# Adding the last layer's output into HBM by accumulating transfers instead of on VectorE

## What is computed

```python
h    = rmsnorm(x, g_ple_pre)
gate = sigmoid(h @ w_ple_gate)            # 2048 x 2048
proj = p @ w_ple_proj                     #  256 x 2048
y    = rmsnorm(gate * proj, g_ple_post)
out  = x + y                              # 256 x 2048, fp32, 2 MB
```

## Time and profile before

| what | value |
|---|---|
| median of the runs | 3245.95 us |
| the profiled execution's own time | 3246.77 us |
| its span, first to last instruction | 3244.8 us |
| TensorE busy | 3213.2 us, 99% |
| VectorE busy | 2093.9 us, 65% |
| ScalarE busy | 1584.2 us, 49% |
| GpSimd busy | 88.6 us, 3% |
| moved by DMA | 596.27 MB, mean 184 GB/s |
| mean granted TensorE clock | 0.998 of full speed |

### The profile page before, as it was taken

One profiled execution on the slowest core, in us unless ns is written; L12 is line 12 of the kernel. 1 busy time (PEld: TensorE's weight loads), 2 busy tenths in 40 slices (PEclk: granted clock), 3 DMA queues, 4 the chain that ended last, 5 costly groups with the idle time before them and its releaser, 6 DMA issues.

```text
span 3244.8 us, 50378 instructions
## 1 busy us (share of the span) xinstructions
PE 3213.2 (99%) x19512; PEld 2846.4 (88%) x19512; DVE 2093.9 (65%) x2258; ACT 1584.2 (49%) x1895; POOL 88.6 (3%) x36
## 2 busy tenths in 40 slices
PE   8999999999999999999999999999999999999997
PEld 7899988888888888888888888999988888888886
DVE  6566677766665557665555456867986655554568
ACT  5445556555454445444444435555644444444354
POOL 0000200000000100000000010000010000000101
PEclk9999999999999999999999999999999999999999
DMA  8545555666666556666656555654556666566654
GB/s 265 177 156 171 190 172 173 194 187 185 193 185 192 188 189 187 190 183 192 187 181 197 190 189 164 220 165 128 178 164 188 186 190 187 179 198 193 189 175 134
DMA packets 324345, 596.27 MB, mean 184 GB/s; under 512 B 18436, under 2 KB 46500, under 8 KB 324196
## 3 DMA queue, kind: packets, MB, share of 16 engines
q1 hardware_dynamic: 316048, 587.27, 58.4%
q10 hardware_dynamic: 8148, 6.90, 0.7%
HBM read 591.97 MB, written 2.13 MB: 183 GB/s over the span
## 4 chain that ended last, share of the span: by engine, by line
PE 95%; DVE 3%; ACT 1%; DMA 1%; issue 0%; POOL 0%; ACTq 0%; DVEq 0%; POOLq 0%
PE acc L715 26%; PE acc L717 25%; PE acc L720 24%; PE acc L775 5%; PE acc L778 4%; PE acc L777 4%; DVE WHL L1830 1%; PE acc L660 1%; PE acc L658 1%; PE acc L659 1%; DMA raw<-in_cmp_k_w 0%; PE acc L596 0%; ACT WHL L1219 0%; PE acc L804 0%; PE acc L963 0%
## 5 line engine op out<-in xcount | busy, mean ns | idle before, releaser
L1830 DVE TENSOR_TENSOR WHL<-raw,WHL 128x1024 fp32r<-128x1024 f32 x1112 | 1384.0, 1255 | 971.6 <-ACT WHL L1219 970.5
L1219 ACT ACTIVATE WHL<-raw 128x1024 fp32r<-128x1024 f32 x1112 | 1164.4, 1057 | 1249.8 <-PE acc L720 992.5
L717 PEld LDWEIGHTS acc<-OPR,WHL 128*128 128x128 f32 x4800 | 903.1, 188 | 199.0
L715 PE MATMUL acc<-OPR,WHL 128*128 128x512 f32 x2556 | 999.9, 397 | 10.8 <-DVE WHL L1830 10.1
L717 PE MATMUL acc<-OPR,WHL 128*128 128x256 f32 x4800 | 971.2, 278 | 0.0
L720 PE MATMUL acc<-OPR,WHL 128*128 128x512 f32 x2244 | 888.3, 396 | 0.0
L715 PEld LDWEIGHTS acc<-OPR,WHL 128*128 128x128 f32 x2556 | 485.5, 190 | 27.9 <-issue 11.3
L717 PEld LDWEIGHTS acc<-HR,WHL 128*128 128x128 f32 x2184 | 410.3, 188 | 94.5
L715 PE MATMUL acc<-HR,WHL 128*128 128x512 f32 x1120 | 440.3, 395 | 0.0
L717 PE MATMUL acc<-HR,WHL 128*128 128x256 f32 x2184 | 433.9, 278 | 0.0
L720 PE MATMUL acc<-HR,WHL 128*128 128x512 f32 x1064 | 420.9, 396 | 0.0
(11 more groups left out here) (390 smaller groups left out, 2288.1 us busy)
## 6 DMA issues: line engine op xcount, KB each, us to landing
raw<-in_w_up SPq DMA_DIRECT2D x176, 512.0 KB, 4.4
raw<-in_ff_w_gate SPq DMA_DIRECT2D x176, 512.0 KB, 3.8
raw<-in_ff_w_up SPq DMA_DIRECT2D x176, 512.0 KB, 4.5
raw<-in_ff_w_down SPq DMA_DIRECT2D x176, 512.0 KB, 4.3
raw<-in_w_in SPq DMA_DIRECT2D x162, 512.0 KB, 4.1
raw<-in_w_down SPq DMA_DIRECT2D x88, 512.0 KB, 3.8
raw<-in_w_out SPq DMA_DIRECT2D x64, 512.0 KB, 4.1
raw<-in_w_ple_gate SPq DMA_DIRECT2D x32, 512.0 KB, 4.8
```

The lines of the kernel that those rows point to most:

```text
L715: pe.matmul(acc[:, b + t, :], wh[:, s, col:col + P], x, start=first, stop=False)
L717: mm = pe.matmul(acc[:, b + t, 0:T], wl[:, s, col:col + P], x[:, 0, :], start=False, stop=last and t % 2 == 0)
L1219: act.activation(wh[:, s, :], raw[:, s, :], ACT.Copy).then_inc(hi_done, 1)
L1830: dve.tensor_tensor(wl[:, s, :], raw[:, s, :], wh[:, s, :].bitcast(F32), ALU.subtract)\
```

## The change

The output gets `X` by one 2 MB transfer, which SP issues between the loads of `ple_gate` and those of `ple_gb` once `X` is final. At the end VectorE only multiplies, in place in `YG`, without the waits on its own results. GpSimd waits for that one store and then, for each group, issues a transfer from `YG` that adds to what the output holds. SP ends the program when the five adding transfers have landed.

```diff
             stream("ple_gate", *plain(a["w_ple_gate_2"]))
+            sp.wait_ge(first_x, 3 * FIRST_X["ple_pre"] + 3)
+            sp.wait_ge(ssq_src, SRC["ple_pre"] + 4)
+            sp.dma_start(out.rearrange("(c p) t -> p c t", p=P), X[:, :, :]).then_inc(out_stored, 16)
             stream("ple_gb", *plain(a["w_ple_gate_2"], 2 * NB))
             stream("ple_pl", *plain(a["w_ple_proj_2"], 3 * NB))
 
-            for n, (first, last) in enumerate(OUT_GROUPS):
-                sp.wait_ge(out_done, n + 1)
-                sp.dma_start(out.rearrange("(c p) t -> p c t", p=P)[:, first:last, :], X[:, first:last, :])\
-                  .then_inc(out_stored, 16)
-            sp.wait_ge(out_stored, 16 * len(OUT_GROUPS))
+            sp.wait_ge(out_added, 16 * len(OUT_GROUPS))
...
             for n, (first, last) in enumerate(OUT_GROUPS):
                 k = last - first
                 dve.wait_ge(y_scaled, first // 4 + 1)
-                if n >= 1:
-                    dve.wait_ge(out_done, n)
-                chain(dve.tensor_tensor(T2[:, 0:k, :], YG[:, first:last, :], bc(RSTD[:, :], k), ALU.mult))
-                dve.tensor_tensor(X[:, first:last, :], X[:, first:last, :], T2[:, 0:k, :], ALU.add).then_inc(out_done, 1)
+                dve.tensor_tensor(YG[:, first:last, :], YG[:, first:last, :], bc(RSTD[:, :], k), ALU.mult)\
+                   .then_inc(out_done, 1)
...
             squares("ple_post", four(HFc, 20, 3), y_done, 1)
+            gp.wait_ge(out_stored, 16)
+            for n, (first, last) in enumerate(OUT_GROUPS):
+                gp.wait_ge(out_done, n + 1)
+                gp.dma_start(out.rearrange("(c p) t -> p c t", p=P)[:, first:last, :], YG[:, first:last, :], accum_op=ALU.add)\
+                  .then_inc(out_added, 16)
```

More of the change, by code:

```diff
@@ L311, in program @@
         pg_pre, pg_sig = sem("pg_pre"), sem("pg_sig")
+        out_added = sem("out_added")
         out_done, y_scaled = sem("out_done"), sem("y_scaled")
```

## The result

The changed kernel takes 3250.53 us, the median of 20 runs between 3249.47 and 3252.28; the kernel before takes 3246.43 us in 20 runs beside them (3245.76 to 3247.36). That is 4.1 us more, a ratio of 1.0013 with a 95% interval of 1.0007 to 1.0018. It is slower, by more than the noise of the comparison but by less than the 6.5 us that the text above counts as a change. The forecast was +3.8 us and 3249.8. The profiled execution took 3249.47 us with a span of 3247.6.

A forecast was written before the change was run, and what follows sets the result against it. VectorE paces the end, the transfers follow. First multiply 3232.75 plus 0.1, 1.8, 0.7, 12.3 and 0.6 gives 3248.2 against 3244.4, or +3.8; early store 0; 3246.0 + 3.8 = 3249.8 us, range 3242 to 3266.

The forecast's parts named there:

- The floor: Kernel's end: last multiply 3236.2 plus 0.1 plus 2.1 us of a small store, -6.0 us at best.
- VectorE's part: Kernel's end: five adds and their waits go; multiplies end 3232.75 to 3236.2, last group ready 6.0 us earlier.
- The start of the block: Adding transfers at the end: after the first multiply, wake-up 0.1, GpSimd's issue 1.8, first packet 0.7, reaching 3235.35.
- The size of the block: Adding transfers at the end: moving the bytes takes 12.3 us, bounded between 6.2 and 36.4 us.
- Two passes: Adding transfers at the end: fetch and write one after the other on each transfer engine, 12.3 us.
- The cover for the issues: GpSimd's later issues hide beside the bytes of earlier ones, up to 3.1 us an issue.
- Rival B: Transfers at the end: adding is as cheap as storing, 6.2 us of bytes; -3.7 us, 3242.3; chance 0.13.
- Rival C: Transfer engines after 3232.85: read-add-write of small rows bound by its own delay; +12.5 to +24.9 us; chance 0.31.
- the likeliest case: Kernel's end: added read halves the rate, adding transfers bound it; 3249.8, with issue varied 3248.4 to 3252.5; chance 0.51.
- The early store: SP's queue after X's last add at 3158.30: the 2 MB store of X fits a gap and costs 0.
- load 17: Weight load behind the 2 MB store: ScalarE takes it at 3169 instead of 3166.65, margin 1 to 2 us.
- Rival D: Near 3175: the 2 MB store of X starves the weight split, TensorE waits; +2 us, 3251.8; chance 0.05.

The follow-up runs named there:

- early_store_alone: The kernel before plus the early 2 MB store of X between the gate's loads, stores at the end unchanged: 3246.66 us beside 3246.32, ratio 1.0000.

## Why the prediction was right

- **The floor and VectorE's part held.** The multiplies took 4.70 us, forecast 4.67, and ended 3.5 us after the first. VectorE stretched nothing while GpSimd issued. The gain that is there to be had, all else plain, was put at -3.7 us and measured at -4.0.
- **The start of the block held, with its parts shifted.** Forecast: 2.6 us from the first multiply to the first packet, as 0.1 of wake-up, 1.8 of issue and 0.7. Measured: about 2.6 us, as 0.65 before the issue starts, 1.43 of issue and 0.55. The wake-up was too short, the issue too long. The issue stood on a midpoint between distant rows. The 0.7 us were read as counted from the start of SP's issue and then added behind GpSimd's; in the trace of the kernel before, SP's first packets come 0.9 us after the start (3234.04 to about 3234.95) and 0.55 after the end of the issue. So that the sum came out is partly luck.
- **The size of the block held.** Forecast 12.3 us, two passes; measured 12.4. But the inside is otherwise: at 195 to 200 GB/s the 2.1 MB would take 10.6 us, and the slow stretches and the end of the block add the rest. Adding into SBUF took 11.05 us. Two passes were chosen as the nearest in kind out of bounds from 6.2 to 36.4 us; the slow start was in no term, so part of the agreement is luck. What the Trainium skill says in "Collectives: The Full Stack", "The bandwidth ceiling: the fold count and why AG ≠ RS ≠ AR", agrees in size: it has an add at about half the rate of a copy, and here it is 197 against some 350 GB/s, or 1.8 times. That it is the second read which costs this, and not the adder, no run here tells apart.
- **The cover for the issues** was claimed up to 3.1 us an issue; GpSimd needed 1.2 to 1.4 and the engines were busy throughout. The rate is flat from 3238.8, when the last issue has ended (3238.60), until 3245.6. Before that it dips to 118 to 167 GB/s for four slices from 3237.2, while the last issue runs. Whether it causes the dip is not shown; it is worth 0.4 us.
- **Rival B** fell with the block, and its number was met by the plain stores of SP instead. **Rival C** would have needed 4.5 us per 512 KB; the block gives 3.1. The upper bound of the likeliest case, 3252.5, does not follow from its terms: 1.4 us more of issue give 3251.2, and issues of 3.2 us each would no longer be covered by 3.1 us of bytes.
- **The early store cost next to nothing, as forecast, with too much cover claimed.** I put load 17 2.4 us later with a margin of 1 to 2 us, and load 18's at about 1. In early_store_alone it came just so. In the changed kernel it came 3.3 us later with margins of 0.5 and 0.3 us, and in two other profiled executions load 18's was gone, for up to 0.2 us of TensorE's time. Rival D was closer than its chance of 0.05 says: 1 MB more cost 3.9 us.

## What to carry to other kernels

Handing an elementwise add at the end of a kernel to the transfer engines can pay only for as much as fits into their idle time: count an adding transfer at twice the time of a store, plus 2.6 us until GpSimd's first packets flow, and compare with the vector engine's time per byte. Here an add of 512 KB costs VectorE 1.45 us with its waits and the engines need 1.5 us more for it; with one group, part of that falls into their idle time and the gain, 1.1 us, is within the noise, with all of them the kernel loses. A big transfer slipped into the queue of a just-in-time weight stream must be judged by the margin of every load behind it, here that of the second, and in more than one execution, since its time differed by 1.3 us between executions. Past that margin the whole of the further delay reached TensorE here, and with a wait of 3.1 us some clock was lost too.

## What was not expected of the hardware

- The first adding transfer of 512 KB into HBM was issued by GpSimd in 1.43 us, the following ones ended 1.2 to 1.3 us apart, also those of 256 KB; plain ones took 0.71 to 0.92. Their records overlap, so the last one's 3.1 us is not its own work alone.
- GpSimd's plain store joined rows of 1 KB into 4 KB packets (592 packets for 2.1 MB), SP's and the adding ones to HBM did not (2128). The rate was about the same for both plain forms.
- An adding transfer into HBM started at 40 to 170 GB/s for about 2 us; into SBUF, with a third of the packets, it started at its full 150 to 240.
- TensorE's granted clock fell to 1.2 GHz for 3.4 us, beginning 1.5 us after it had resumed from a wait of 3.1 us. In the changed kernel, with a wait of 0.17 us there, it did not.
